# The output gates' projection in an mLSTM stage: eight matmul blocks spread over 17 steps in place of 13

## The reference, cut to what matters

```python
hm = mlstm_chunkwise(mq, mk, mv, i_pre, log_f)          # 4 heads, values 128 wide
hm = hm * lax.rsqrt(jnp.mean(hm * hm, axis=-1, keepdims=True) + NORM_EPS)
hm = (hm.reshape(B, S, MLSTM_WIDTH) * mlstm_norm).astype(h.dtype)
y_ml = jax.nn.sigmoid(mo) * hm                          # mo = h @ w_in[:, 2336:2848]
return jnp.concatenate([y_nsa, y_ml], axis=-1) @ w_out
```

## Time and profile before

| | us |
|---|---|
| median of three executions | 1813.83 |
| the profiled execution | 1812.71 |
| its span | 1810.9 |
| PE busy | 1756.3 (97%) |
| DVE busy | 892.5 (49%) |
| ACT busy | 618.5 (34%) |
| POOL busy | 126.6 (7%) |

### The profile page before, as it was taken

One profiled execution on the slowest core, in us unless ns is written; L12 is line 12 of the kernel. 1 busy time (PEld: TensorE's weight loads), 2 busy tenths in 40 slices (PEclk: granted clock), 3 DMA queues, 4 the chain that ended last, 5 costly groups with the idle time before them and its releaser, 6 DMA issues.

```text
span 1810.9 us, 25668 instructions
## 1 busy us (share of the span) xinstructions
PE 1756.3 (97%) x10733; PEld 1323.9 (73%) x10733; DVE 892.5 (49%) x1843; ACT 618.5 (34%) x1080; POOL 126.6 (7%) x82
## 2 busy tenths in 40 slices
PE   6999999997999999999999999999999999999998
PEld 5877867886655555555578967667888788888786
DVE  4355554453365555655563577655725532222323
ACT  3334465432111111111252456654624422222222
POOL 1000110221000000000000000011101000000121
PEclk9999999998999999999999999999999999999999
DMA  6511200458999999999926312013421133313201
GB/s 248 203 47 49 92 24 24 140 201 352 409 410 426 426 426 427 426 425 425 398 102 227 113 51 68 1 47 128 163 94 58 48 117 109 109 50 140 93 24 47
DMA packets 76225, 333.55 MB, mean 184 GB/s; under 512 B 6184, under 2 KB 13992, under 8 KB 63177
## 3 DMA queue, kind: packets, MB, share of 16 engines
q1 hardware_dynamic: 72472, 325.04, 45.8%
q0 software_dynamic: 2336, 4.20, 0.6%
q10 hardware_dynamic: 1296, 2.62, 0.4%
HBM read 325.55 MB, written 10.49 MB: 186 GB/s over the span
## 4 chain that ended last, share of the span: by engine, by line
PE 89%; DVE 5%; ACT 3%; issue 1%; DMA 1%; POOL 0%; SPq 0%; DVEq 0%; POOLq 0%; ACTq 0%
PE ps L561 86%; PE ps L980 1%; PE ps L3014 1%; DVE splitr L626 1%; PE ps L2131 1%; DVE arenaf L3096 1%; ACT arenaf L969 0%; DVE arenaf L3114 0%; DMA arenaf<-in_w_out 0%; ACT splitr L637 0%; DVE xf L3405 0%; PE ps L815 0%; DMA xf<-in_x 0%; POOL hr L912 0%; DVE hr L869 0%
## 5 line engine op out<-in xcount | busy, mean ns | idle before, releaser
L561 PE MATMUL ps<-hr,splitr 128*128 128x512 f32 (+1 forms) x2784 | 572.8, 365 | 7.0 <-POOL hr L912 3.8
L561 PEld LDWEIGHTS ps<-hr,splitr 128*128 128x128 f32 x2784 | 471.8, 191 | 87.9 <-issue 6.0
L561 PE MATMUL ps<-splitr,hr 128*128 128x512 f32 (+1 forms) x1488 | 273.9, 343 | 1.0 <-DVE hr L1077 0.8
L561 PEld LDWEIGHTS ps<-splitr,hr 128*128 128x128 f32 x1488 | 234.2, 190 | 34.5 <-DVE hr L1077 1.2
L626 DVE TENSOR_TENSOR splitr<-ring,splitr 128x2048 fp32r<-128x2048 f32 x61 | 142.8, 2342 | 213.0 <-ACT splitr L637 212.9
L2251 DVE TENSOR_TENSOR xf<-xf,ps 128x512 f32<-128x512 f32 x248 | 153.5, 681 | 67.3 <-PE ps L561 67.2
L561 PE MATMUL ps<-arenaf 128*64 128x256 f32 (+7 forms) x1424 | 176.4, 360 | 2.6 <-ACT arenaf L790 1.7
L637 ACT CAST splitr<-ring 128x2048 fp32r<-128x2048 f32 x61 | 116.1, 1906 | 144.4 <-PE ps L561 143.1
L2205 ACT ACTIVATE junkr<-ps,arenaf 64x512 fp32r<-64x512 f32 x62 | 42.3, 682 | 287.8 <-PE ps L561 287.0
L561 PEld LDWEIGHTS ps<-arenaf 128*64 128x64 f32 (+2 forms) x1424 | 107.6, 150 | 43.9 <-issue 12.5
L626 DVE TENSOR_TENSOR splitr<-arenaf,splitr 128x2048 fp32r<-128x2048 f32 x27 | 62.4, 2310 | 101.8 <-ACT splitr L637 101.8
(11 more groups left out here) (421 smaller groups left out, 1960.3 us busy)
## 6 DMA issues: line engine op xcount, KB each, us to landing
arenaf<-in_w SPq DMA_DIRECT2D x23, 2048.0 KB, 15.9
ring<-in_w SPq DMA_DIRECT2D x22, 2048.0 KB, 15.3
splitf<-in_w SPq DMA_DIRECT2D x20, 2048.0 KB, 15.4
hf<-in_w SPq DMA_DIRECT2D x20, 2048.0 KB, 16.4
ring<-in_w_in SPq DMA_DIRECT2D x11, 2048.0 KB, 12.0
otf<-in_w SPq DMA_DIRECT2D x11, 2048.0 KB, 15.4
ring<-in_w_gate_up SPq DMA_DIRECT2D x7, 2048.0 KB, 7.9
arenaf<-in_w_in SPq DMA_DIRECT2D x4, 2048.0 KB, 9.1
```

Of the source, the lines that this page charges most:

```text
L561: return te.matmul(out, lhsT, rhs, start=start, stop=stop)
```

## The change

Two numbers change: the eight blocks are dealt over the first 17 steps, and the extra move of the walk on ACT and DVE goes from step 13 to step 17.

```diff
             def ml_beats(s):
-                return share(8, 13, s)
+                return share(8, 17, s)
...
                         if u == 13:
                             powers(14)
                             powers(15)
-                        go(beats, ml_beats(u) + (u == 13))
+                        go(beats, ml_beats(u) + (u == 17))
                         for what, k in ML_SIDE.get(u, []):
                             se_ml_side(what, k)
...
                     if part == "beat":
-                        go(beats, ml_beats(u) + (u == 13))
+                        go(beats, ml_beats(u) + (u == 17))
                         for what, k in ML_SIDE.get(u, []):
                             ve_ml_side(what, k)
```

## The result

The changed kernel took 1821.49 us in the median of seven executions (1819.11 to 1826.75), the kernel before 1813.83 us. The ratio is 1.0038, with a 95% interval of 1.0025 to 1.0051: slower by 7 us. Run again later beside the kernel before on one chip, it took 1821.37 against 1814.79 us, ratio 1.004 (1.0027 to 1.0053). The forecast was 1820, with a range of 1814 to 1824.5.

The account below looks back on a forecast made before the run. PE, busy for 97% of the span, was taken as the bound. Waits +6.8, old clock loss -6.8 and new clock loss +6.8 gave +6.8 us: 1819.5 on the profiled time, 1820.6 on the median, stated as 1820, range 1814 to 1824.5.

Parts of the forecast that it names:

- Step 1: Early mLSTM steps: two blocks fewer before the fourth head's row, which starts 5.6 us earlier; 0.1 us of new wait.
- Step 2: Step 12: w_out's cast and low part delay "times" of head 0; PE idles 2.9 us more, bounds 0 to 4.2.
- Step 3: Steps 14 to 17: split 0's cast waits for block 8; PE idles 4.7 us, 3.8 more, bounds 2.8 to 4.6.
- Step 4: Behind block 8: head 3's spread waits up to 1.0 us at full clock, 0 at half clock; taken as 0.
- Step 5: Other moves (low part of og's second piece, key weights' DMA, load of w_out's second half): 0 each.
- Step 6: Clock falls behind two longer waits, steps 13 and 16 to 17; 6.8 us lost, bounds 3.4 to 10.2, old 6.8 gone.
- B: Rival: the waits come but low clock falls mostly inside them; +3.4 us, 1817; chance 0.25.
- C: Rival: blocks 7 and 8 hold the clock at 1.00 while the waits come; +1.0 us, 1814.8; chance 0.11.
- D: Rival: blocks 7 and 8 fill the three old waits and hold the clock; -8.4 us, 1805.5; chance 0.07.

Follow-up runs that it names:

- second profile: Profile of the changed kernel run again without edit beside the kernel before; median 1821.37 us, ratio 1.0040, profiled execution 1821.05 us.
- first profile: Profile of the changed kernel's first run, its slowest execution of seven at 1826.75 us; median 1821.49 us, ratio 1.0038 to the kernel before.
- both: Changed kernel with the four splits moved behind block 8 and w_out's first piece prepared in step 9; 1812.05 us, ratio 0.9984 to the kernel before.
- table first: Mended kernel with DVE's low part of split 2 moved behind the table of head 2; 1809.99 us, ratio 0.9977 to the kernel before.
- splits late: Changed kernel with splits 0 and 1 moved to step 17, 2 and 3 to step 18; 1815.94 us, ratio 1.0009 to the kernel before.
- filler: Changed kernel with six needless fp32 products on PE, three ahead of C(10), three ahead of C(14); 1817.45 us, ratio 1.0015 to the kernel before.
- mended kernel: Changed kernel, w_out's first piece after step 10's side work, splits ending step 16 and in step 17, last og copy in step 18; 1809.35 us, ratio 0.9968.
- weights late: Kernel before with the cast and low part of w_out's first piece in step 12 instead of step 9; 1820.32 us, ratio 1.0026.

## Why the prediction was right, and where it was not

*Step 1, the early steps.* It held. No wait over 0.2 us stands ahead of the fourth head's row. From the first row to the fourth there are 35.55 us in the second profile, against 40.88 before: 5.3 us less, for 5.6 forecast. In the first profile it was 37.15, because of a low stretch of 3.42 us that has no wait ahead of it. I had tied low clock to waits alone and had not allowed for this one; it cost 1.7 us. PE was busy ahead of it, but for 2.9 us with small matmuls alone (64x512, a transpose, the row of 4x512, 64x128); the same ones stand there in the second profile, where the clock stayed at 1.00. The profiles of "both" and "table first" have the early stretch too.

*Step 2, the weights.* Forecast 2.9 us more at C(10) (its own rows, 1216.6 - 1213.57, give 3.0), measured 3.21 - 0.36 = 2.85, with the chain of rows as foretold. Taking the weights back removed it, and moving them alone, with no block moved, made it. Shown.

*Step 3, the split that waits for block 8.* Forecast about 1, 2.7 and 1.0 us, 4.7 in sum; measured 0.87, 2.90 and 0.58 or 0.93, which is 4.4 to 4.7. Moving the splits behind block 8 removed all three. Shown. One bound was wrong: with B(15) done first the chain is 1.91 us shorter, which leaves 2.8 us of idle time, but only 1.9 more than the 0.92 of before, and the bound for "more" says 2.8. The central figure does not use it.

*Step 4, the tail.* Forecast 0 while the clock is low there: no wait stood at head 3's spread in either profile of the changed kernel. With the clock full it does wait: 0.64 us with the splits late, 0.94 with filler; 1.0 was the forecast for that case. In the mended kernel it does not wait, with the clock full, since PE had already waited 1.90 us at head 2's spread.

*Step 5, the other moves.* They were put at 0, and no wait over 0.2 us stands on PE up to the fourth head's row.

*Step 6, the clock.* Forecast a loss of 6.8 us, as much as before, in two stretches, one behind each of the two waits. The second profile has exactly that. The first one has 12.0, over the bound of 10.2: a long stretch behind each wait, and the short early one that has no wait ahead. The prediction named a third fall and its price of 1.7 us, though with a short idle time as its cause. The sum of +6.8 us stands against 6.6 in the stage of the second profile (8.19 - 1.55 = 6.6 of waits, 0 of clock) and 6.6 to 7.7 in the medians. That the clock's change came out at 0 is in part luck: no row decided for the pair that was taken out of those that give 3.4 to 10.2 us. The mechanism was half right. In the changed kernel the clock fell behind both long waits in both profiles, and with the waits filled by dense work the loss went to 0. But "each of the waits brings a fall" did not hold in the other kernels: with both repairs mended, PE waited 0.36, 0.27 and 1.90 us in the profiled execution and never lost the clock, and with the table first it lost it twice, once with no wait ahead. So the length of a wait does not decide by itself, and the same program differs between executions.

*The rivals.* B (the clock costs little) and C (the blocks keep it up) were not the changed kernel. C's picture, the clock at 1.00 throughout, is what the mended kernel's profile shows, once the waits of 3.21 and 2.90 us are gone. D priced the faster outcome at -8.4 us and named the two conditions, that "times" is not late and that the split does not hold up ACT and DVE. With both conditions made true, the time was 5.4 us less than before. D's condition was right and its price too high, as it counted all waits as gone, and 2.5 us of them stay. What stays open is why the clock fell in one execution and not in another of the same program; no experiment here separates that.

## What to carry to other kernels

When a list of side work is respread by one number, look at every walk that the number drives: here PE's blocks could move at no loss once the rest was put right, and the cost came from a cast and a subtraction of weights that moved with them, and from one wait on the last block that stood at the head of two in-order engines. Price such a wait by what is queued behind it, and move the waiting instruction with what it waits for. With both put right, the spread kernel was 5.4 us faster than before; in its profiled stage, 5.6 us shorter, the clock gave back 6.8 us and longer waits took 1.0. Whether the spread of the blocks earned that is not shown: the mended order of splits and weights was never run with the blocks at their old places. What speaks for the spread is that needless dense products at the new places of blocks 7 and 8 halved the clock's loss in the profile of the kernel before, from 6.8 to 3.4 us.

## What the runs showed of the hardware

The clock took only two levels in these stretches. The low ones differed in length: 3.42, 10.22 and 10.25 us in one profile of the changed kernel, 6.82 twice in the other, and 13.65 with the weights late. The level 0.50 is 1.2 GHz and 1.00 is 2.4 GHz. A block took 3.01 us with the clock full (row 1248.35, above) and 5.00 us from 1223.16, where 4.31 us of it lay in a low stretch: half of 4.31 and the 0.69 behind it make 2.85.

DVE instructions that read two tensors from SBUF were stretched while POOL worked on its own subtraction. In the mended kernel the table of head 2 took 1.55 us beside POOL's 1.38 us at 1227.03 (above), and the same instruction took 0.69 us in the changed kernel, and so the spread of head 2 waited some 0.9 us longer, by estimate from these two figures. The Trainium skill's page "SBUF — State Buffer", section "SBUF: two separate sides", says that a DVE instruction with two SBUF inputs and a POOL instruction that reads SBUF take turns at a shared port, one whole instruction at a time. The trace agrees in kind: POOL still had 1.00 us to go when the table started, and 1.00 and 0.69 are 1.69, for 1.55 measured. In the changed kernel's first profile the order was the other way round: the table started at 1243.01, with POOL idle, and took 0.69 us, while POOL's subtraction started at 1243.35 and took 1.48 us, where the one at 1236.30 had taken 1.26.
